# The last gate tile of a 2-layer decoder step, spread over steps 2 to 4 of the last head pair

## The reference

```python
def nsa_query_side(x, g_pre, w_in):
    u = rms_norm(x, g_pre) @ w_in
    q = u[..., :Q_WIDTH]                                     # 16 heads x 64
    z = u[..., Q_WIDTH:Q_WIDTH * (1 + N_BRANCH)]             # 3 branches x 16 heads x 64
    gate = sigmoid(u[..., Q_WIDTH * (1 + N_BRANCH):])

def nsa_output(x, o, z, gate, w_out, g_post):
    y = sum(gate[..., None] * o * silu(z), axis=2)           # over the branches
    return x + rms_norm(y @ w_out, g_post)
```

## Time and profile before

| | |
|---|---|
| median of three runs | 965.39 us |
| the profiled execution | 964.63 us, its span 962.8 us |
| mean granted TensorE clock | 0.984 |
| TensorE busy | 907.4 us, 94% of the span |
| VectorE, ScalarE, GpSimd busy | 531.0, 437.5, 307.0 us |
| DMA | 97.43 MB, mean 101 GB/s |

### The profile page before, as it was taken

How to read it: one execution, slowest core, us unless ns; L and a number is a source line. 1 busy time by engine, 2 the same in 40 slices (tenths; PEclk the granted TensorE clock), 3 DMA queues, 4 the chain that set the end, 5 groups by cost and what they waited for, 6 DMA issues and landing times.

```text
span 962.8 us, 16757 instructions
## 1 busy us (share of the span) xinstructions
PE 907.4 (94%) x6278; PEld 771.3 (80%) x6278; DVE 531.0 (55%) x1171; ACT 437.5 (45%) x895; POOL 307.0 (32%) x313
## 2 busy tenths in 40 slices
PE   3899999998999999999979999999999999799995
PEld 2899999944479877778979898989898898686653
DVE  3479999965943572332135545545554645545563
ACT  4556777524412532233245545545454646423421
POOL 1479888661470000003012331322232233400000
PEclk9899999999999999999979999999999999999997
DMA  7446433157336143166132222313222101922521
GB/s 208 106 122 186 112 99 90 36 173 278 136 106 235 45 155 86 25 142 194 32 89 44 67 46 65 88 26 87 45 67 54 36 2 38 277 73 92 174 78 34
DMA packets 156071, 97.43 MB, mean 101 GB/s; under 512 B 97156, under 2 KB 144932, under 8 KB 155911
## 3 DMA queue, kind: packets, MB, share of 16 engines
q1 hardware_dynamic: 141134, 77.07, 29.9%
q0 software_dynamic: 4896, 10.32, 3.0%
q10 hardware_dynamic: 9961, 8.97, 2.9%
HBM read 87.48 MB, written 18.85 MB: 110 GB/s over the span
## 4 chain that ended last, share of the span: by engine, by line
PE 84%; ACT 4%; SPq 4%; DMA 3%; DVE 3%; issue 2%; POOL 0%; DVEq 0%; ACTq 0%
PE psum L1746 9%; PE psum L2079 7%; PE psum L2080 6%; PE psum L2081 6%; PE psum L1765 6%; PE psum L1766 6%; PE psum L1767 6%; PE psum L2174 5%; PE psum L2144 4%; PE psum L2109 4%; PE psum L2127 3%; PE psum L1999 3%; PE psum L1998 3%; PE psum L2000 3%; PE psum L1842 3%; ACT arena L1171 3%
## 5 line engine op out<-in xcount | busy, mean ns | idle before, releaser
L2079 PE MATMUL psum<-u_hi,tile_hi 128*128 128x288 f32 x464 | 147.0, 317 | 8.6 <-ACT arena L767 8.4
L767 ACT ACTIVATE arena<-psum 128x512 f32<-128x512 f32 (+9 forms) x214 | 82.2, 434 | 144.7 <-PE psum L2000 48.7
L746 POOL TENSOR_SCALAR arena<-arena,kept 128x512 f32<-128x512 f32 (+3 forms) x128 | 83.6, 670 | 183.0 <-DVE kept L1612 183.0
L2080 PE MATMUL psum<-u_lo,tile_hi 128*128 128x288 f32 x464 | 138.4, 298 | 0.0
L2081 PE MATMUL psum<-u_hi,tile_lo 128*128 128x288 f32 x464 | 137.6, 296 | 0.0
L1321 DVE SCALAR_TENSOR_TENSOR psum<-arena,psum 128x512 f32<-128x512 f32 x168 | 127.0, 756 | 6.0
L1765 PE MATMUL psum<-h_hi,tile_hi 128*128 128x288 f32 x352 | 104.4, 297 | 0.0
L1766 PE MATMUL psum<-h_lo,tile_hi 128*128 128x288 f32 x352 | 104.2, 296 | 0.0
L2079 PEld LDWEIGHTS psum<-u_hi,tile_hi 128*128 128x128 f32 x464 | 88.3, 190 | 19.8 <-ACT arena L767 11.4
L1767 PE MATMUL psum<-h_hi,tile_lo 128*128 128x288 f32 x352 | 103.9, 295 | 0.0
L1543 DVE COPY arena<-psum 128x512 f32<-128x512 f32 (+3 forms) x72 | 37.0, 514 | 103.1 <-PE psum L2127 100.4
(11 more groups left out here) (291 smaller groups left out, 1837.9 us busy)
## 6 DMA issues: line engine op xcount, KB each, us to landing
tile_whole<-in_b_w_in SPq DMA_DIRECT2D x64, 256.0 KB
tile_whole<-in_a_w_in SPq DMA_DIRECT2D x24, 512.0 KB
arena<-in_cmp_w SPq DMA_DIRECT2D x3, 2048.0 KB, 9.8
kvw_whole<-in_w_kv SPq DMA_DIRECT2D x6, 1024.0 KB, 11.3
bias_copies<-bias_line POOLq DMA_DIRECT2D x4, 1280.0 KB, 23.7
arena<-in_x_prompt SPq DMA_DIRECT2D x8, 512.0 KB, 10.1
arena<-in_a_w_out SPq DMA_DIRECT2D x4, 1024.0 KB, 16.6
arena<-bias_copies SPq DMA_DIRECT2D x16, 256.0 KB, 3.7
```

The costliest lines, as they stand in the source:

```text
L746: pool.tensor_scalar(L, L, rden[:, stat(n) + k:stat(n) + k + 1], gR[:, i, h:h + 1], ALU.mult, ALU.mult).then_inc(S["pn_ready"], 1)
L767: return nc.scalar.activation(out, in_, ACT.Copy, scale=scale)
L2079: pe.matmul(pb(7, HT), w_hi, u_hi[:, k, here], start=(k == 0), stop=False)
L2080: pe.matmul(pb(7, HT), w_hi, u_lo[:, k, here], start=False, stop=False)
```

## The change

For the last pair (n // 5 = 7) the table is replaced by a list of its own: nothing in step 35, half 0 of the last tile in step 36, the first four k of half 1 in step 37, the other four in step 38, nothing in step 39, each in the first slot. ScalarE's drain of a half moves along with its last k, and so does the point at which SyncE may load the output weights. The order of the halves and all else stay.

```diff
@@ -361,6 +361,8 @@
             if n >= 5 * KD:
                 return (None, None)
             first = AHEAD + 4 * (n // 5)
+            if n // 5 == KD - 1:
+                return (None, (first, 0, range(KD)), (first, 1, range(4)), (first, 1, range(4, KD)), None)[n % 5], None
             return [(first + i, hf, range(lo, hi)) if first + i < N_TILES else None for i, hf, lo, hi in PARTS[n % 5]]
```

## The result

The changed kernel takes 968.75 us (median of 20 runs, 966.25 to 973.74) against 966.72 us before (20 runs, 964.08 to 968.44): a ratio of 1.0025, interval 1.0014 to 1.0037. It is 2.0 us slower: inside the predicted range, and within the 0.3% that the prediction counted as no change, its likeliest outcome (0.69). Of the prediction's three terms the rearrangement came in at its size here, the clock's loss only in later executions of the same kernel, and the queue, costed at nothing, took about 1 us.

The account below looks back on a forecast made before the run. The prediction took TensorE to bound the kernel, busy nearly the whole span. Rearrangement +0.8 us and clock +1.5 us, with late weights at nothing, summed to +2.3: 967.7 us from the median 965.39, range 964.9 to 969.6.

Parts of the forecast that it names:

- the rearrangement: Steps 35 to 39: moving the tile's matmuls alone costs +0.8 us; bounds -0.46 and +2.9.
- Step 35, tile gone: Step 35: four turns start at 806.22, 2.06 us earlier, after a new TensorE pause of 2.8 us for ScalarE.
- Step 36: Step 36: a whole half (3.29 us) stands there; turns of step 35 begin at 812.46, leaving 0.46 us of the gain.
- Steps 37 and 38: Late steps, quarters ahead of the holes: 0.26 us lost by scores of step 38, 0.76 by those of step 39.
- The clock, +1.5 us: TensorE after step 35's new pause: clock falls to half speed, costing 1.5 us; bounds nothing and 3.4 us.
- rival 1: Step 35: the clock doesn't fall; then +0.8 us, 966.2; chance 0.30.
- The weights behind it: SyncE queue: output weights and rows behind them go 9.8 us later, but no wait; costed at nothing.
- Rival 4: Output product: late weights stall it by 3 us; then +3.8 us, 969.2; chance 0.07.
- The sum: Whole kernel: +0.8 rearrangement and +1.5 clock make +2.3 us, 967.7 from the median.
- Rivals 2 and 3: Late steps: 2, clock stays half longer, 969.6, chance 0.12; 3, quarters vanish in holes, clock holds, 964.9, chance 0.06.

Follow-up runs that it names:

- second slot: Changed kernel with the tile's pieces in the second slot of steps 36 to 38, between first and second turns: 971.47 us against 967.32 before, 1.0047.
- both, again: Repeat: changed kernel with the pieces between first and second turns and new value rows ahead of gains and residual rows: 967.72 us against 966.95 before, 1.0013.
- the best version: Changed kernel, tile pieces in second slots of steps 35 to 38, second and third weight chunks loaded first, new value rows earlier: 963.95 us against 966.47 before, 0.9969.
- the filled one: Changed kernel plus 16 needless matmuls in the hole of step 35: 969.23 us against 966.47 before (1.0028); again 969.61 against 966.95 (1.0027).
- pause pieces: Changed kernel with the tile's pieces in the second slots of steps 35 to 38, the first in the pause: 965.91 us against 966.47 before, 0.9990.
- late weights: Kernel before, tile where it was, only output weights' loads and all behind them on SyncE start later: 969.96 us against 967.32 before, 1.0024.
- rows first: Changed kernel with the first four new value rows issued ahead of gains and first residual rows on SyncE: 970.15 us against 967.32 before, 1.0029.

## Why the prediction was right, point by point

- **Step 35, tile gone.** Six turns at once, a hole of 2.63 us (worked: 2.8), the four turns at 806.01 (806.22). Right. This trace begins 0.12 us earlier by the first score of step 35, so the two marks agree within 0.1 us.
- **Step 36.** Turns of step 35 at 812.26 (812.46): 0.5 us left of the 2.06. Right.
- **Steps 37 and 38.** Scores of 38 at 818.57 (818.7), of 39 at 824.58 (824.5). The rearrangement costs 36.87 - 35.90 = 0.97 us for +0.8 worked. The reason, the slot ahead of the hole, is shown by the second slot, where the same quarters cost nothing. In the first slot about half of their 2 x 1.69 us was hidden: two steps became 1.50 us longer (11.79 against 10.29).
- **The clock, +1.5 us.** In the profiled execution it did not fall, so there rival 1 was true. In six of seven executions with this hole it fell, and cost 1.5 to 1.6 us. Right in mechanism and size by stage. How much of it stands in the median is open, see below.
- **The weights behind it, "I cost it at nothing".** This step failed. The weights were never late. But the prediction let cache and residual rows "go 9.8 us later too" without pricing their reader: the first transposes also wait for the new value rows, behind all of these in the queue. With the late queue and the old order of these rows the product stage took 0.2 to 2.5 us more in all eight executions, 0.9 to 1.2 in the three of the changed kernel. The right term was about +1. Rival 4 had the kind of loss, with the wrong transfer.
- **The sum.** +2.3 forecast, +2.0 measured in the first set, +1.5 and +3.7 in the two others. By stages the loss at the first cache transposes is 0.97 + 0.93 = 1.9 us where the clock held (55.64 against 53.74 after the scores of step 35) and 3.7 where it fell (57.48 both times). Nearly all of it reaches the end: from the first cache transposes to the end of the span are 109.11 us before and 108.70 and 108.73 in the two executions with the fall; the 110.93 of the first execution hold the later fall at 893.8. Most executions should then lose 3 us or more, and the medians lost 1.5 to 3.7. What makes up the difference is not settled: the clock also falls at other places that change from one execution to the next (231 us in some, 893 or 922 us in two), and only one execution of each run was profiled. The mean granted clock of each execution explains only part of the scatter: longer times go with lower clocks, strongly in "both, again" (correlation -0.90 over 12 executions), weakly in the kernel before of the first set of experiments (-0.37 over 29). So the closeness of the total, +2.0 for +2.3, is in part luck: a term of about +1 was missing, and the clock's +1.5 did not show whole in the median. In the one profiled execution of that measurement it was not there at all.
- **Rivals 2 and 3.** No half-clock stretch near the hole lasted longer than 3.4 us. The holes did not swallow the quarters in the first slot; in the second they did.

## What to carry to other kernels

Here a wait that shows as idle time was filled at no cost only by work placed between the instruction that starts the wait and the one that ends it; one slot earlier the same work also delayed the start, and only about half of it was hidden. Before moving work away, look at what it covered: here it hid a ScalarE chain of table loads and silus, and the best version put nearly as much work back as the hole was long (a hole of 0.24 us was left). And when the end of a stage moves, follow the DMA queue behind it to the last transfer that a later semaphore counts, not only to the first.

## What the runs showed of the hardware

An 8 KB transfer from SBUF to SBUF, issued behind some megabytes on the same queue, held its reader until 10.0 to 11.6 us after its issue, in the eight traces whose chain of waits names it. Two executions of one kernel, the filled one, differ by more than 1 us in this (10.03 and 11.12 us).

A pause of TensorE of 2.63 us inside otherwise full work was enough for the granted clock to fall to 0.50 in six of seven executions, while pauses of 1.21 to 1.44 us in the same stage never did. In front of the cache transposes a pause of 2.28 us lost the clock (pause pieces), and pauses of 2.10 (late weights) and 1.75 us (second slot) did not. The length alone does not decide: in the output stage a pause of 1.22 us was followed by a fall about 2 us after its end in two executions (891.78 in the changed kernel, 920.29 in rows first), and the same pause before (889.95) was not. Whether these pauses caused the falls is not shown.
